# Delta rule and product-key selection: where output splits, key rows, value transposes and the first scores stand in the order of work

## What is computed

```python
# first block, after attention: product-key retrieval of experts
q = (xb @ wq).reshape(128, 8, 2, 64)             # 4 token tiles of 128, 8 heads, 2 halves
s1 = einsum('thd,hnd->thn', q[:, :, 0], keys[:, 0]); s2 = ...   # 128 keys a half
v1, i1 = top_k(s1, 16);  v2, i2 = top_k(s2, 16)
cand = v1[..., :, None] + v2[..., None, :]       # 256 candidates a head
sc, ci = top_k(cand, 16);  g = softmax(sc)
e = i1[ci // 16] * 128 + i2[ci % 16]
out = sum_k gelu(u[e] . x) * g * v[e]

# second block, layer 0: gated delta rule, 16 value heads of 128, 9 chunks of 64 positions
a = strict_lower(k_beta @ k.T * decay)           # per chunk and head
sol = triangular_solve(a + eye, [v * beta, k_beta * exp(cum)])
for chunk: v_new = u - w @ S;  o = q_dec @ S + attn @ v_new;  S = S * last + k_dec.T @ v_new
o = rms_norm(o) * silu(z);  h = h + o @ w_out
```

## Time and profile before

| | |
|---|---|
| median of 3 runs | 3917.52 us (3915.14 to 3923.86) |
| the profiled execution | 3911.82 us, of it span 3910.0 us |
| TensorE matmul busy | 3644.2 us (93%), 24325 matmul records |
| VectorE, ScalarE, GpSimd busy | 2510.8 (64%), 1519.7 (39%), 762.4 us (19%) |
| mean granted TensorE clock | 0.967 of full speed |
| query products | about 560 to 610 us |
| selection and one-hot | 612 to 1139 us |
| delta rule | about 1880 to 2800 us |

### The profile page before, as it was taken

How to read it: one execution, slowest core, us unless ns; L and a number is a source line. 1 busy time by engine, 2 the same in 40 slices (tenths; PEclk the granted TensorE clock), 3 DMA queues, 4 the chain that set the end, 5 groups by cost and what they waited for, 6 DMA issues and landing times. The chain is left out here.

```text
span 3910.0 us, 60019 instructions
## 1 busy us (share of the span) xinstructions
PE 3644.2 (93%) x24325; PEld 3397.9 (87%) x24325; DVE 2510.8 (64%) x5009; ACT 1519.7 (39%) x2704; POOL 762.4 (19%) x658
## 2 busy tenths in 40 slices
PE   7999999999979999999888899998899999979999
PEld 5777879999978999999788888887799999968999
DVE  5664346998978888989576666666543434565342
ACT  4555333335643333333434333332432334444241
POOL 0000004775423333332121221111000011010000
PEclk9999999999999999999899999998899999999999
DMA  3112224677879898988252332221132212112221
GB/s 120 60 65 72 91 90 135 235 233 234 272 240 342 319 346 322 338 323 317 54 79 47 59 60 54 59 51 41 50 99 91 92 44 66 62 53 81 95 95 60
DMA packets 208147, 542.29 MB, mean 139 GB/s; under 512 B 18664, under 2 KB 92904, under 8 KB 207872
## 3 DMA queue, kind: packets, MB, share of 16 engines
q1 hardware_dynamic: 99792, 341.22, 25.3%
q0 software_dynamic: 42048, 150.49, 13.8%
q10 hardware_dynamic: 66032, 46.75, 3.8%
HBM read 492.14 MB, written 46.25 MB: 138 GB/s over the span
## 5 line engine op out<-in xcount | busy, mean ns | idle before, releaser
L104 PE MATMUL bank<-Xh,wh 128*128 128x256 f32 (+3 forms) x3680 | 1225.6, 333 | 40.8 <-DVE Xl L131 21.0
L104 PE MATMUL bank<-Xl,wh 128*128 128x256 f32 (+3 forms) x3680 | 1161.1, 316 | 0.0
L104 PE MATMUL bank<-Xh,wl 128*128 128x256 f32 (+3 forms) x3680 | 1160.4, 315 | 0.0
L125 ACT ACTIVATE wh<-raw 128x1024 fp32r<-128x1024 f32 (+1 forms) x632 | 587.7, 953 | 681.4 <-PE bank L104 582.3
L131 DVE TENSOR_TENSOR wl<-raw,wh 128x1024 fp32r<-128x1024 f32 (+1 forms) x539 | 573.9, 1083 | 422.1 <-ACT wh L125 418.5
L104 PEld LDWEIGHTS bank<-Xh,wh 128*128 128x128 f32 x3680 | 710.6, 193 | 109.2 <-issue 63.1
L104 PEld LDWEIGHTS bank<-Xl,wh 128*128 128x128 f32 x3680 | 711.3, 193 | 17.9
L104 PEld LDWEIGHTS bank<-Xh,wl 128*128 128x128 f32 x3680 | 708.2, 192 | 20.8
L131 DVE TENSOR_TENSOR H<-H,bank 128x256 f32<-128x256 f32 (+3 forms) x394 | 182.8, 469 | 314.2 <-PE bank L104 312.1
L104 PE MATMUL bank<-aah,wh 128*128 128x384 f32 x1024 | 349.7, 341 | 13.9 <-DVE wl L131 12.3
L104 PE MATMUL bank<-aal,wh 128*128 128x384 f32 x1024 | 347.5, 339 | 0.0
(11 more groups left out here) (337 smaller groups left out, 6038.9 us busy)
## 6 DMA issues: line engine op xcount, KB each, us to landing
raw<-in_u SPq DMA_DIRECT2D x128, 512.0 KB, 3.8
raw<-in_v SPq DMA_DIRECT2D x128, 512.0 KB, 5.4
raw<-in_up SPq DMA_DIRECT2D x64, 512.0 KB, 3.4
raw<-in_down SPq DMA_DIRECT2D x64, 512.0 KB, 3.3
scratch<-gb ACTq DMA_DIRECT2D x12, 2048.0 KB, 11.1
gj<-scratch SPq DMA_DIRECT2D x32, 768.0 KB, 8.3
raw<-in_w_gdn SPq DMA_DIRECT2D x48, 512.0 KB, 3.4
raw<-in_w_att SPq DMA_DIRECT2D x36, 512.0 KB, 3.3
```

Of the source, the lines that this page charges most:

```text
L104: return Issued(self, self.q and self.q.matmul(out, l, r, start=start, stop=stop), 1)
L125: return Issued(self, self.q.activation(out, in_, func, **kw), 1)
```

## The change

Two groups of edits.

Selection: the scores and the top-16 of both halves for token tiles 0 and 1 are made head by head (`first_scores`, `first_top`) between the query products, the last head after three steps of `neurons_ahead`. `top16(tl, s)` for s below 2 remains for tiles 2 and 3; `VV` and `II` become double; the second half of `SS` shares its memory with `CA`; the declared cost of `select` falls by 46.

Delta rule: `gdn_split` of pair p - 1 stands behind scan steps 0 and 1 of pair p; the gate buffer is given back there. The key rows `ke` are scaled by ScalarE (three activations a group) instead of VectorE. The value transposes and `bv` go from `pair` to level 3. GpSimd writes the even (unit) columns of `tb` once a pair, VectorE the odd ones in `pair`, and `level0` stands directly behind them. GpSimd's `queries` wait for `tb` of level 1.

```diff
+        def first_scores(h):
+            for s in range(2):
+                PA.take(("ks", "first", h, s))
+            do("first_scores", h)
+            for s in range(2):
+                PA.give(("ks", "first", h, s), ("ss", h, s))
+        ws = [query_begin(h) for h in range(3)]
+        dense_together([WQ[h] for h in range(3)])
+        done_with(ws[0], WQ[0])
+        for h in range(3):
+            query_end(h)
+        for h in (1, 2):
+            done_with(ws[h], WQ[h])
+        first_scores(0)
+        do("first_top", 0)
+        for h in range(3, 8):
+            s = query_begin(h)
+            for k, _ in enumerate(dense(WQ[h])):
+                if h == 3 and k in (2, 4):
+                    first_scores(k // 2)
+                    do("first_top", k // 2)
+            done_with(s, WQ[h])
+            query_end(h)
+            if h > 3:
+                first_scores(h - 1)
+                do("first_top", h - 1)
...
-                for s in range(2):
+                for s in range(2 if tl > 1 else 0):
                     do("top16", tl, s)
...
-                    yield from some_early(tl, 2)
+                    yield from some_early(tl, 2 if tl > 1 else 3)
+                    if tl == 0:
+                        scores_of(2, s)
...
-        merge((neurons_ahead(0, 4 * AHEAD - HELD), 9 * (4 * AHEAD - HELD)),
-              (select(), 4 * 60 + 1.25 * ROWS_EARLY + 5 + NT // 8 * ONEHOT))
+        ahead = neurons_ahead(0, 4 * AHEAD - HELD)
+        for _ in range(3):
+            next(ahead)
+        first_scores(7)
+        do("first_top", 7)
+        merge((ahead, 9 * (4 * AHEAD - HELD)),
+              (select(), 4 * 60 - 46 + 1.25 * ROWS_EARLY + 5 + NT // 8 * ONEHOT))
...
             do("keys_twice", p)
+            do("unit_columns", p)
...
-                for n in ("kk", "vt"):
-                    PA.take((n, p, g))
+                PA.take(("kk", p, g))
                 do("pair", p, g)
-                PA.give(("vt", p, g), ("bv", p, g))
...
                 do("keys_out", p, g)
-                PA.give(("ke", p, g), ("ke", p, g))
-                do("level0", p, g)
+                PA.give(("ke", p, g), ("kout", p, g))
...
+                    if lv == 3:
+                        PA.take(("vt", p, g))
+                        do("values_out", p, g)
+                        PA.give(("vt", p, g), ("bv", p, g))
...
-            for e in range(2):
-                do("gdn_split", p, e, None)
-                yield 1
-            out_ready.add(p)
             VD.give(p, ("og", p, 2, 1))
-            ZG.give(p, ("ogl", p, 1))
+
+        def out_split(p, e):
+            do("gdn_split", p, e, None)
+            if e:
+                out_ready.add(p)
+                ZG.give(p, ("ogl", p, 1))
...
                 yield 1
+                if p and c < 2:
+                    out_split(p - 1, c)
...
# VectorE, pair
+                dv.tt(odd, three(BB, g)[:, :, 1:128:2], b3(CS["lev0"])[:, :, 1:128:2], ALU.mult)
+                dv.tt(odd, b3(IDENT)[:, :, 1:128:2], odd, ALU.subtract)
+                dv.squares(three(TA, g)..., tb...)
# ScalarE, keys_out
+                for c in range(3 * g, 3 * g + 3):
+                    i = ac.act(ke[:, c, :], PS[...][:, (c - 3 * g) * 128:(c - 3 * g + 1) * 128],
+                               ACT.Copy, scale=LC[:, c, p:p + 1])
# GpSimd
+                po.wait_ge("tb", p, 1, g)        # queries
-                po.tt(three(tb, g), three(BB, g), b3(CS["lev0"]), ALU.mult)
-                po.tt(three(tb, g), b3(IDENT), three(tb, g), ALU.subtract)
+                po.tcopy(tb[:, :, 0:128:2], IDENT[:, 0:128:2]...)     # unit_columns
```

More of the change, by code:

```diff
@@ L858, in build @@
         do("keys")
-        WQ = {}
-        for hs in ((0, 1, 2), (3,), (4,), (5,), (6,), (7,)):
-            ss = [slab("w_q", h) for h in hs]
-            for h, s in zip(hs, ss):
-                WQ[h] = group(PD, by_slab(s), of_x(16, 528), 512, lambda k: xn2(16, k))
-            dense_together([WQ[h] for h in hs])
-            for h, s in zip(hs, ss):
-                done_with(s, WQ[h])
-                do("query", h)
-                given_back(WQ[h], "query", h)
-        SS = alloc("ss", 16, 128)
+        SS = alloc("ss", 2, 16, 128)
+        CA = SS[:, 1].rearrange("p (h x) k -> p h (x k)", h=8)
         S2_AT = top[0]
@@ L873, in build @@
         EQ = alloc("eq", 128, 16)
-        VV = alloc("vv", 2, 8, 16)
-        II = alloc("ii", 2, 8, 16)
-        CA = alloc("ca", 8, 256)
+        VV = [alloc("vv", 2, 8, 16) for _ in range(2)]
+        II = [alloc("ii", 2, 8, 16) for _ in range(2)]
         CV = alloc("cv", 8, 16)
@@ L890, in build, with query_begin, query_end @@
         assert top[0] <= S_AT
+        WQ = {}
+        def query_begin(h):
+            s = slab("w_q", h)
+            WQ[h] = group(PD, by_slab(s), of_x(16, 528), 512, lambda k: xn2(16, k))
+            return s
+        def query_end(h):
+            do("query", h)
+            given_back(WQ[h], "query", h)
+        def first_scores(h):
[24 more added lines that the diff above has]
+                do("first_top", h - 1)
         top[0] = S_AT
@@ L2034, in values, with first_scores @@
                 x.then_inc("val", u, i, m)
+            def first_scores(h):
+                ps = [PS[clear(pe, PA, ("ks", "first", h, s))] for s in range(2)]
+                pe.wait_ge("query", h)
+                pe.wait_ge("keys", 0)
+                for n in range(4):
+                    tl, s = n // 2, n % 2
+                    i = pe.mm(ps[s][:, tl * 128:(tl + 1) * 128],
+                              QP[s * 64:s * 64 + 64, h, tl * 128:(tl + 1) * 128], KEY[s * 64:s * 64 + 64, h, :])
+                    if tl:
+                        i.then_inc("ks", "first", h, s)
             def key_scores(tl, s, hh):
@@ L2426, in merge, with first_top @@
                 dv.tt(MGL[:, fb, :], t, MGH[:, fb, :].bitcast(F32), ALU.subtract).then_inc("ml", fb)
+            def first_top(h):
+                dv.wait_ge("ss", h, 1)
+                jobs = [(n // 2, n % 2, SS[:, n // 2, n % 2 * 8 + h, :], S2[4 * (h % 2) + n][:, 0:128],
+                         VV[n // 2][:, n % 2, h, :], II[n // 2][:, n % 2, h, :].bitcast(U32)) for n in range(4)]
+                for tl, w, src, rest, v, i in jobs:
+                    dv.max8(v[:, 0:8], src).then_inc("top_a", tl, w, h)
+                for tl, w, src, rest, v, i in jobs:
+                    dv.wait_ge("top_a", tl, w, h)
+                    dv.max_index(i[:, 0:8], v[:, 0:8], src).then_inc("top_b", tl, w, h)
+                for tl, w, src, rest, v, i in jobs:
+                    dv.match_replace(rest, v[:, 0:8], src).then_inc("top_c", tl, w, h)
+                for tl, w, src, rest, v, i in jobs:
+                    dv.wait_ge("top_c", tl, w, h)
+                    dv.max8(v[:, 8:16], rest).then_inc("top_d", tl, w, h)
+                for tl, w, src, rest, v, i in jobs:
+                    dv.wait_ge("top_d", tl, w, h)
+                    dv.max_index(i[:, 8:16], v[:, 8:16], rest).then_inc("top", tl, w, h)
             def top16(tl, w):
@@ L2430, in top16 @@
                     dv.wait_ge("ss", tl, w, 1)
-                    jobs = [(SS[:, w * 8 + h, :], VV[:, w, h, :], II[:, w, h, :]) for h in range(8)]
+                    jobs = [(SS[:, 0, w * 8 + h, :], VV[tl % 2][:, w, h, :], II[tl % 2][:, w, h, :]) for h in range(8)]
                 else:
@@ L2435, in top16 @@
                 n = 128 if w < 2 else 256
-                if tl and w == 0:
+                if tl and w == (0 if tl > 1 else 2):
                     dv.wait_ge("picked", tl - 1, 1)
@@ L2991, in fixed, with first_scores @@
                 ac.copy(ps[:, 0:128], iota).then_inc("fixed")
+            def first_scores(h):
+                for s in range(2):
+                    ac.wait_ge("ks", "first", h, s)
+                    ac.copy(SS[:, :, s * 8 + h, :],
+                            PS[PA.at["ks", "first", h, s]][:, 0:256].rearrange("p (t k) -> p t k", t=2)).then_inc("ss", h, s)
             def key_scores(tl, s, hh):
                 a0 = s * 8 + hh * 4
-                if tl:
-                    ac.wait_ge("top", tl - 1, s, 7)
+                ac.wait_ge("top", 0 if tl == 2 else 2, s, 7)
                 ac.wait_ge("ks", tl, s, hh)
-                ac.copy(SS[:, a0:a0 + 4, :], PS[PA.at["ks", tl, s, hh]].rearrange("p (a b) -> p a b", a=4)).then_inc(
+                ac.copy(SS[:, 0, a0:a0 + 4, :], PS[PA.at["ks", tl, s, hh]].rearrange("p (a b) -> p a b", a=4)).then_inc(
                     "ss", tl, s, hh)
```

65 lines of the change are left out of this document (35 added, 30 removed).

## The result

| | before | after |
|---|---|---|
| median of the runs | 3916.97 us (3915.14 to 3923.86) | 3865.38 us (3860.71 to 3869.40) |
| the profiled execution | 3911.82, span 3910.0 | 3865.24, span 3863.4 |
| mean granted TensorE clock | 0.967 | 0.971 |

The ratio is 0.9865, interval 0.9849 to 0.9881: 51.6 us faster. The forecast was 69.5 us, with 3812 to 3892 us as the range. So the sign is right, the time lies inside, and a quarter of the gain is missing. In the code after, the helpers' lines are one higher (L105 is every matmul, L108 a transpose, L126 an activation, L132 tensor_tensor, L142 scalar_tensor_tensor, L149 a copy).

What follows compares the result with a forecast made beforehand. TensorE was taken to bound the kernel, except where VectorE works through a burst at each delta-rule step's front. Delta rule -58.5 us and selection -11 us made -69.5, from 3917.5 to 3848.0 us; 8-in-10 range 3812 to 3892.

Steps and rivals of the forecast that it cites:

- terms 1 to 5: Front of a delta-rule step: `tb`, key, value, `qe` and beta edits take 40 of 44.2 us off the `ta` wait.
- Rival C: Delta rule, level 3: value transposes compete for five banks and TensorE stalls; slower, 3975 us, chance 0.06.
- Rival D: Delta-rule front: row and beta transfers set it, so the change doesn't act; 3914 us, chance 0.05.
- those for right: Signs: `ta` under 8 us, step 96 to 98, stage clock 0.96, one-hot products 893 to 1129, two gates 1.5 us.
- those for wrong: Signs: new `st`, convolution or bank waits, odd-column operations over 1 us, slab 6 stall, longer idle front at t = 8.
- Rival A: Delta rule: VectorE's burst itself is the bound, not its order; only its shortening is won, 3889 us, chance 0.17.
- Term 13: Selection, before one-hot products: VectorE ends 25 us sooner; 5.4 of 7.1 us idle go, and 3 us of half clock.
- term 10: Delta rule: work late behind old stalls is late behind the next; +2 us in six steps, +12, bounds 0 and +30.
- terms 1 to 7 and 10: Delta-rule waits: -40 us on `ta`, -8 on `vn`, -3 on `dd` and banks, -3.5 on `vd`, +12 for renewed lateness.
- Term 8: Delta-rule clock: TensorE's time at the lower level shrinks with the idle places; -20 us, bounds 0 and -35.
- Terms 6, 7 and 9: Delta rule: moved output splits -8 us; `dd` and bank waits -3, `vd` -3.5; late output buffer at t = 8 +4.
- term 7: Delta rule: TensorE's `dd` and bank waits fall by 3 us, its `vd` wait by 3.5 us.

Runs made afterwards that it cites:

- e7: Changed kernel with both `tb` operations on GpSimd again and `level0` behind the key copies; ratio to the kernel before 0.9924, 19.5 us slower than the changed kernel.
- e8: Changed kernel without the wait of GpSimd's `qe` multiplications for level 1; ratio to the kernel before 0.9913, 15.7 us slower than the changed kernel.
- e2: Kernel before with the selection edits alone; ratio 0.9970, 11.6 us faster than the kernel before.
- e1: Kernel before with the delta-rule edits alone; ratio 0.9909, 37.7 us faster than the kernel before.
- e4: Changed kernel with gates 1 and 2 behind scan steps 0 and 1, splits behind 2 and 3, for five pairs; ratio to the kernel before 0.9827.
- e9: e4 with ScalarE's query-convolution silu and squares, and key-norm sums and inverse root, three dense steps later; ratio to the kernel before 0.9772.
- e3: Changed kernel with both output splits ahead of the scan again; ratio to the kernel before 0.9874, 51.3 us faster than that kernel.
- e6: Changed kernel with value transposes and their scaling at the front again; ratio to the kernel before 0.9869, 2.0 us slower than the changed kernel.
- e5: Changed kernel with key rows scaled by VectorE again; ratio to the kernel before 0.9877, 5.3 us slower than the changed kernel.
- e12: Kernel before with only e11's reordering; `tb`, keys, values, `qe` and selection as before; ratio 0.9907, 36.9 us faster than the kernel before.
- e10: e4 with gate 0 also behind scan step 0, and splits ahead of the scan for p above 4; ratio to the kernel before 0.9795.
- e11: e4 with the edits of both e9 and e10; ratio to the kernel before 0.9753, 95.3 us faster.

## Why the prediction was right in kind and 18 us too large

**What was right.** The bound (TensorE, with VectorE's burst behind its idle places); terms 1 to 5 (`ta` gone altogether, 0.36 us an odd operation, 0.39 us of beta wait, 0.35 us a gate); the worth of `tb` on VectorE with `ta` ahead (e7: 19.5 us) and of the `qe` wait (e8: 15.7 us); the selection (-11 forecast, -12 measured between the starts of the delta rule). Rival C (banks at level 3, 3975 us) didn't come: no wait of that kind is in the list. Rival D (no effect, 3914 us) is refuted by the time, 3865 us.

**Which signs came.** Of those for right there came `ta`, the two gates, the first one-hot product (894) and the last (1127, with 1129 forecast); missed were a step of 96 to 98 us (101.0) and a clock of 0.96 in the stage (0.95). Of those for wrong one came: t = 8 is longer than before (68.8 against 62.4 us). What the forecast said for Rival A misreads the trace: VectorE isn't without a pause from 2332 to 2349, it stands idle for the last 2.69 us of that, waiting for ScalarE's `ogh`.

**Inside the selection** one number fell otherwise than drawn. Term 13 let VectorE be ready at 893.3 us and TensorE at 891.8, with 5.4 of 7.1 us idle time won. The products began at 894.05, but TensorE was there at 887.9, so 6.18 us of idle time remain, and the 5.4 us of term 13 weren't won there. The stretches from 612 to 1139 in the result section show where the gain was made instead. TensorE's idle time in the four fell from 33.2 to 30.5 us, and what the clock cost (one less the clock, times the length) from 14 to 8 us. So 2.6 us are idle time (4.6 less in the tail, 2.0 more ahead of it), and some 6 us are clock, by clocks of two digits, where the forecast had 3. That makes about 9 of the 12.8 us won at the last product in this profile. The stretches are the same times and not the same work, and what was won ahead of 612 us isn't in them. No slab was late near 600 us.

**The step that failed is term 10.** The forecast took +2 us a step for work that "will be late behind the next one", from the 2.44 us of ScalarE's convolution wait, with a bound of +30 in all. What came is `st` 2.5, `rt` 1.8, `vd` 1.1 and `rc` 1.1 us: 6.4 us a step. Idle time fell by 3.1 us a step, where terms 1 to 7 and 10 together, -42.5 us in seven steps, make 6.1. The pair e2 and e1, which have the same steady steps as before and after, gives 8.8 and 6.8 us, a fall of 2.0. In other words, Rival A was a part of the truth: the burst bounds the step up to the last operation that TensorE needs from it, and I had followed it only up to `ta`. e4 shows this for `st`: moving 1.4 us of gates and the two splits out of the front, with no work taken away, brought 3.3 us a step. The waits on `rt` and `vd`, 2.9 of the 6.4 us, are not VectorE's but the order of ScalarE's own list, as e9 shows, where both are gone.

**Term 8**, the clock, was -20 us for the stage, 2.9 us in each of seven steps. From the granted clock of the four steps it is 0.05 x 106.7 = 5.3 us lost before and 0.04 x 101.0 = 4.0 after: 1.3 us a step. But the clock of the same steps varies between executions. The same view of e2, with the steps of the kernel before, and of e1, with those of the kernel after:

```profile
2136.01:2562.53 426.52, 388.69 (x2954) 360.76 (x2953) 292.73 (x605) 156.24 (x328) 82.10 (x100) 0.94 0.30 57
```

```profile
2125.02:2528.34 403.32, 377.58 (x2952) 352.04 (x2952) 281.06 (x618) 168.10 (x365) 61.42 (x80) 0.97 0.30 60
```

This pair makes it 0.06 x 106.6 = 6.4 less 0.03 x 100.8 = 3.0, so 3.4 us a step, at the same lengths of the step. Between 1.3 and 3.4 us the term may have been right or less than half there; one profile of each kernel can't tell. With more of the gaps gone, the clock was 0.98 in e4 and 1.00 in e9.

**Terms 6, 7 and 9.** The splits were given -8 us, mostly in the steady steps. e3 shows 0 there; they bring 8.7 us between the first two state copies, and cost 5.5 us at t = 8 and 2.2 behind it, where +4 was forecast for the late output buffer. Net: some 1 us in the profiles and nothing that the times can tell. Of term 7 the part on `vd` (-3.5) failed outright: that wait is 5.9 us now instead of 4.2, for another reason (ScalarE's late silu). The part on `dd` (-3) came in the steady steps, where its 0.7 us a step are gone, but outside them these waits rose by more than that.

**The sum for the stage**, from profile to profile, state copy to state copy: four steady steps -22.7; the step ahead of them 118.1 to 102.6, -15.5; the one behind 103.3 to 96.8, -6.4; t = 8 62.4 to 68.8, +6.4; beginning and end together -2.0. That is -40.2, where -58.5 was forecast. Four steps at the forecast 97 us would have brought another 16 us: nearly all of the missing 18.

**What stays open.** Why e6 costs so little wasn't tested. Of the 5.7 us by which a step fell, 3.1 are idle time, 1.3 the clock, and 1.3 have no row that names them; by e2 and e1 it is 5.8, of it 2.0 idle time, 3.4 the clock and 0.4 left. So how the gain divides between idle time and clock stays open. The waits on `rc`, 1.1 us a step, are not explained: e3 alone of the runs on the changed kernel has none in its steady steps. Whether the key copies on ScalarE help (e5, 5.3 us) is within the intervals.

## What to carry to other kernels

When a burst on one engine holds another, follow it to the last result in it that the other engine needs, not to the first one that is late: the time won is the wait of today less the wait on the next name, and each item behind in the same queue is a candidate. If work may be spread, first take out of the burst what nobody is waiting for (here the gates and splits, 15 us, then one silu and one norm, 20 us more) before making its operations cheaper: in e12 such moves alone brought 37 us, as much as the change's own edits in this stage. And check the last iterations apart: an order that cost nothing in the steady steps (a buffer given back late) cost 5.5 us where there was no other dense work.

## What the runs showed of the hardware

- Contention between VectorE and GpSimd doesn't slow an operation in proportion: a 0.36 us operation took 3.47 us (e8), from just ahead of the start to the end of three multiplications on GpSimd that lasted 2.94 us. The price there is the length of GpSimd's work, as with the gates of the kernel before (3.71 us instead of 0.73, beside 3.06 us). Not every operation pays. In e12 a scaling that reads a bank and a transpose kept their usual time beside the same three multiplications:

```profile
2229.19 0.55 DVE L131 TENSOR_TENSOR ke<-bank,lc 128x384 f32<-128x384 f32 x1
2229.66 0.56 DVE L171 STREAM_TRANSPOSE ta<-tb 128x384 f32<-128x384 f32 x1
```

```profile
2228.83 3.41 POOL L131 TENSOR_TENSOR qe<-qk,qe 128x384 f32<-128x384 f32 x3
```

- The granted clock of four steps rose from 0.95 to 0.96, 0.98 and 1.00 as the idle time of a step fell from 9.6 to 6.4, 5.4 and 3.0 us. These are after's, e4's and e9's values; e10 had 1.00 at 4.9 us and e11 0.98 at 2.3 us, so within 0.02 it isn't the sum of the gaps alone that sets it. Executions of one kernel differ too: nine of the kernel before, beside e9 to e11, had a mean clock of 0.960 to 0.967 over the whole time, at 3927 to 3913 us. What came back beside the idle time is of the same size as the idle time itself (2.0 beside 1.1 us from the changed kernel to e4, 2.0 beside 2.4 from e4 to e9; from clocks of two digits, so each 2.0 is good to 1 us).
- A change of ScalarE's function table took 1.28 us, with the activation 0.01 us behind it; it is longer than four copies of 128 columns (0.28 us each), and where one stood ahead of the activation that was to free a bank for TensorE (`rt`), it was 1.28 of the 1.75 us that TensorE waited.
